# Low-rank products moved into the last pair of the first attention, latent norm applied as scales

## The reference

```python
u = rmsnorm(h, attn_norm_g)
proj = u @ w_in                       # 3*512 + 256 + 128 + 64 columns
q_sb, k_sb, v_sb, c_q, c_kv, k_rope = split(proj)
# 8 heads of 64: stick-breaking attention on q_sb, k_sb, v_sb
# latent attention, 4 heads: 128 plain and 64 rotated columns in q and k, 128 in v
q_m = rmsnorm(c_q, q_a_norm_g) @ w_q_b     # 256 -> 4 * (128 + 64)
kv  = rmsnorm(c_kv, kv_a_norm_g) @ w_kv_b  # 128 -> 4 * (128 + 128)
q_rope, k_rope = apply_rope(...)
s = (q_nope . k_nope + q_rope . k_rope) * MLA_SCALE, causal; p = softmax(s); o = p @ v
```

## Time and profile before

| | us |
|---|---|
| three runs | 3790.58, 3791.27, 3786.0 |
| median | 3790.58 |
| span of the profiled execution, first to last instruction | 3784.3 |
| own time of the profiled execution | not listed apart from the three runs |
| TensorE busy | 3616.2 (96% of the span) |
| VectorE, ScalarE, GpSimd busy | 1805.3, 1216.1, 1341.8 |
| mean granted TensorE clock | 0.980 of full speed |

### The profile page before, as it was taken

One profiled execution on the slowest core, in us unless ns is written; L12 is line 12 of the kernel. 1 busy time (PEld: TensorE's weight loads), 2 busy tenths in 40 slices (PEclk: granted clock), 3 DMA queues, 4 the chain that ended last, 5 costly groups with the idle time before them and its releaser, 6 DMA issues. The chain is left out here.

```text
span 3784.3 us, 48486 instructions
## 1 busy us (share of the span) xinstructions
PE 3616.2 (96%) x17484; PEld 2956.1 (78%) x17484; DVE 1805.3 (48%) x3405; ACT 1216.1 (32%) x2273; POOL 1341.8 (35%) x800
## 2 busy tenths in 40 slices
PE   7997898999999999999999999998999999999997
PEld 6776677888888888788888888886888686868686
DVE  4666544244444445566666666666303424242412
ACT  4777243200000003455545555556101202020200
POOL 3211201233333222565565566563333131313331
PEclk9997899999999999999999999998999999999998
DMA  3100101111111113432222422211413020202231
GB/s 95 29 12 6 42 31 73 56 62 46 49 50 50 46 34 79 56 52 51 53 51 48 37 40 36 37 37 56 150 51 100 28 73 23 78 23 73 95 133 67
DMA packets 201142, 208.81 MB, mean 55 GB/s; under 512 B 12479, under 2 KB 155886, under 8 KB 200958
## 3 DMA queue, kind: packets, MB, share of 16 engines
q1 hardware_dynamic: 181390, 155.23, 17.5%
q10 hardware_dynamic: 19568, 50.93, 3.7%
HBM read 174.61 MB, written 31.52 MB: 54 GB/s over the span
## 5 line engine op out<-in xcount | busy, mean ns | idle before, releaser
L877 PE MATMUL ps<-all_u_hi,kept_w_hi 128*128 128x512 f32 x1952 | 784.7, 402 | 1.8 <-PEq L486 1.8
L881 PE MATMUL ps<-all_u_hi,kept_w_lo 128*128 128x512 f32 x1952 | 763.1, 391 | 0.0
L880 PE MATMUL ps<-all_u_lo,kept_w_hi 128*128 128x512 f32 x1952 | 761.3, 390 | 0.0
L827 POOL CAST kept_w_hi<-kept_w_raw 128x1024 fp32r<-128x1024 f32 x116 | 127.2, 1096 | 1210.1 <-PE ps L877 710.5
L1554 POOL TENSOR_SCALAR even_probs<-even_probs,even_stat 128x640 f32<-128x640 f32 (+1 forms) x250 | 428.0, 1717 | 347.8 <-DVE even_stat L1995 347.8
L881 PEld LDWEIGHTS ps<-all_u_hi,kept_w_lo 128*128 128x128 f32 x1952 | 366.7, 188 | 79.2
L877 PEld LDWEIGHTS ps<-all_u_hi,kept_w_hi 128*128 128x128 f32 x1952 | 368.5, 189 | 67.9 <-POOL sb_w_lo L829 2.0
L880 PEld LDWEIGHTS ps<-all_u_lo,kept_w_hi 128*128 128x128 f32 x1952 | 368.1, 189 | 66.2
L1811 ACT ACTIVATE even_probs<-even_probs,even_stat 128x128 f32<-128x128 f32 (+7 forms) x256 | 199.1, 778 | 300.8 <-DVE even_stat L1989 300.8
L829 POOL TENSOR_TENSOR kept_w_lo<-kept_w_raw,kept_w_hi 128x1024 fp32r<-128x1024 f32 x116 | 285.3, 2459 | 9.3
L877 PE MATMUL ps<-kept_w_hi,all_u_hi 128*128 128x512 f32 x640 | 250.5, 391 | 7.6 <-DVEq L2874 7.2
(11 more groups left out here) (417 smaller groups left out, 7267.5 us busy)
## 6 DMA issues: line engine op xcount, KB each, us to landing
kept_w_raw<-in_even_w_in_dram SPq DMA_DIRECT2D x64, 512.0 KB, 7.4
kept_w_raw<-in_odd_w_in_dram SPq DMA_DIRECT2D x48, 512.0 KB, 3.8
kept_w_raw<-in_w_up_dram SPq DMA_DIRECT2D x16, 512.0 KB, 4.0
mlp_w_raw<-in_w_up_dram SPq DMA_DIRECT2D x16, 512.0 KB, 4.0
kept_w_raw<-in_w_down_dram SPq DMA_DIRECT2D x16, 512.0 KB, 3.5
mlp_w_raw<-in_w_down_dram SPq DMA_DIRECT2D x16, 512.0 KB, 3.5
scratch_h<-residual SPq DMA_DIRECT2D x8, 1024.0 KB, 4.6
residual<-scratch_negc ACTq DMA_DIRECT2D x16, 512.0 KB, 5.5
```

Source lines behind the costliest of these rows:

```text
L827: nc.gpsimd.tensor_copy(hi, raw).then_inc(w_hi.sem, 1)
L877: ins = nc.tensor.matmul(dst, lh, rh, start=first, stop=False)
L880: nc.tensor.matmul(dst, lh, rl, start=False, stop=False)
L881: return nc.tensor.matmul(dst, ll, rh, start=False, stop=last)
```

## The change

- `stick_stage` also runs the five low-rank units: `following(h)` no longer ends with the last pair, and `LAST_PIECES` gives pair 3 its 40 eighths, two in most steps. They use the same `DENSE` bank. Halves 0 to 5 (c_q, c_kv) are evicted by ScalarE into X[0..2]; halves 6 to 9 by VectorE (`rope_half`), which rotates the key at once.
- The angle chain and the two sines move to the opening of `stick_stage`; ScalarE loads the table for exp and ln behind its last eviction there.
- The latent weights are three more units in the raw slots of the attention's weights. Two are split into the slots of `w`, the third into tile 3 of `UH` and `UL` after the last dense product. Rotated columns are laid out by the loads (many DMAs of 32 or 64 columns) instead of GpSimd copies.
- The 12 identity transposes at the end of the stage, `low_stage` and `turn_norm_stage("nc")` are gone. Both latent gains join the first stage's gain loads (two more DMAs).
- `heads_stage` begins by splitting the unnormalised latents times gain (ScalarE `CH`, VectorE `CL`), squares them, sums the squares over partitions with 24 one-column matmuls between jobs 3 and 4, spreads the key root over partitions with 8 matmuls ahead of the key jobs, and has 5 banks for jobs in place of 8. Keys are evicted by VectorE with a multiplication by the spread root, values by ScalarE with a scale per position. The query root goes into the scale of the latent attention's exponential and its bound.

```diff
+        LAST_PIECES = [2] * STEPS
+        LAST_PIECES[3] = LAST_PIECES[9] = LAST_PIECES[15] = LAST_PIECES[21] = 1
+        LAST_PIECES[22] = LAST_PIECES[23] = 0
...
         def following(h):
-            p = h // STEPS + 1
-            return p if p < rounds else None
+            return h // STEPS + 1
...
+                sp.dma_start(pos, positions.rearrange("b s -> (b s)").partition_broadcast(P))\
+                    .then_inc(step_pos.sem, 16)
+                sp.dma_start(rf[:], tables["rope"]).then_inc(step_pos.sem, 16)
...
+                for v, unit in enumerate(low_units + latent_units):
+                    w_load(sp, w, rounds + v // per, per, v % per, unit)
...
+                first = per * (rounds + 1)
+                for n in (first, first + 1, first + 3, first + 4):
+                    split_unit(n)
+                split(first + 2, *latent_kv)
...
-                    for e in eighths_at(h) if nxt else ():
+                    for e in eighths_at(h):
                         if e % 4 == 0:
                             pe.wait_ge(dense_out.sem, dense_out.at(ND * nxt + e // 4))
...
                 weigh(3 * NCY - 1)
-                turn_ident(DENSE[:, 0:P], 12)
...
                     if n == 1:
                         split_of(0, 0, 0)
+                        act.wait_ge(step_dve.sem, step_dve.at(9))
+                        nc.scalar.activation(RS, A, ACT.Sin).then_inc(step_act.sem, 1)
                     elif n == 3:
                         split_of(0, 0, 1)
+                        act.wait_ge(step_dve.sem, step_dve.at(18))
+                        nc.scalar.activation(RC, B, ACT.Sin).then_inc(step_act.sem, 1)
+                load_exp_and_ln()
...
-                    if nxt and s:
-                        for e in eighths_at(h - 1):
-                            if e % 4 == 3:
-                                take_half(nxt, e // 4, DENSE)
+                    if s:
+                        for n in halves_ended(h - 1):
+                            if nxt < rounds or n not in ROPE_HALVES:
+                                take_half(nxt, n, DENSE)
...
+                def rope_half(n):
+                    i, half = divmod(n - 2 * per, 2)
+                    at = slice(half * HALF, (half + 1) * HALF)
+                    dve.wait_ge(dense_done.sem, dense_done.at(ND * rounds + n + 1))
+                    if i == 0:
+                        nc.vector.tensor_tensor(KR[:, at], DENSE, RC[:, at], ALU.mult).then_inc(dense_out.sem, 1)
+                        return
...
+                    nc.vector.tensor_tensor(TMP[:], DENSE, RS[:, at], ALU.mult).then_inc(dense_out.sem, 1)
...
+                    nc.vector.tensor_tensor(KR[:, at], KR[:, at], TMP[:], ALU.add).then_inc(rot_step.sem, 1)
```

In `heads_stage` (TensorE, then ScalarE, then VectorE):

```diff
+        PIECES = [(0, 0), (1, 0), (0, 1), (1, 1), (2, 0), (2, 1)]
...
-        BANKS = 8
+        BANKS = 5
+        SPREAD, SUMS = 5, 7
...
+                    pe.wait_ge(squares.sem, squares.at(LATENTS))
+                    for s, tiles in enumerate((range(QT), range(QT, LATENTS))):
+                        for t in range(TT):
+                            for k in tiles:
+                                last = nc.tensor.matmul(ps[:, SUMS, s * TT + t:s * TT + t + 1],
+                                                        SQ[:, k, t * P:t * P + P], ones[:, 0:1],
...
+                    if n == 4:
+                        sums_of_squares()
+                    if n == ON_DVE[0]:
+                        spread()
...
+                for k, half in PIECES:
+                    nc.scalar.activation(CH[:, k, at], C[:, k, at], ACT.Copy,
+                                         scale=gain_cols[:, 5 * KT + k:5 * KT + k + 1]).then_inc(hi_done.sem, 1)
+                for k in range(LATENTS):
+                    nc.scalar.activation(SQ[:, k, :], C[:, k, :], ACT.Square).then_inc(squares.sem, 1)
...
+                rope(0, 0)
+                rope(0, 1)
+                rope_lo(0)
+                dve.wait_ge(stats_done.sem, stats_done.at(1))
...
+                rstd_chain_dve(dve, v, r, q)
...
+                rope(1, 0)
+                rope(1, 1)
+                for t in range(TT):
+                    nc.vector.tensor_scalar(R[:, t * P:t * P + P], ident[:], KV_ROOT[:, t:t + 1], None, ALU.mult)\
+                        .then_inc(turn_scaled.sem, 1)
+                rope_lo(1)
+                nc.vector.tensor_tensor(KRL, KR[:], KRH.bitcast(F32), ALU.subtract).then_inc(split_lo.sem, 1)
+                for n in ON_DVE:
+                    dve.wait_ge(spread_out.sem, spread_out.at(half + 1))
+                    dve.wait_ge(dense_done.sem, dense_done.at(n + 1))
+                    nc.vector.tensor_tensor(KN[:, j, at], ps[:, n % BANKS, :], R[:, at], ALU.mult)\
+                        .then_inc(part_done.sem, 1)
```

In `latent_stage`:

```diff
-                    nc.scalar.activation(p, p, ACT.Exp, scale=MLA_SCALE, bias=nb[:, s], accum_out=tot[:, s])\
+                    nc.scalar.activation(p, p, ACT.Exp, scale=Q_SCALE[:, t:t + 1], bias=nb[:, s], accum_out=tot[:, s])\
...
-                    nc.vector.tensor_scalar(nb[:, s], top_[:, s], -MLA_SCALE, None, ALU.mult)\
+                    nc.vector.tensor_scalar(nb[:, s], top_[:, s], NEG_Q_SCALE[:, qt:qt + 1], None, ALU.mult)\
```

More of the change, by code:

```diff
@@ L462, in turn_norm_stage @@
         xt = resident if src is None else sb("x", [P, TT, W])
-        NG = NK + len(more) * KT
+        rows_of_more = [sum(n // P for n, _ in more[:i]) for i in range(len(more) + 1)]
+        NG = NK + rows_of_more[-1]
         gain_rows = sb("gain_rows", [NG, P])
@@ L952, in stick_stage @@
         ND = 2 * per
-        KN, QN, VN = (sb(name, [P, SEQ]) for name in ("k_next", "q_next", "v_next"))
+        KN, QN, VN, RC, RS = (X[:, i, :] for i in range(5))
         NEXT = (KN, QN, VN)
@@ L1354, in _ @@
                     s = h % STEPS
+                    if nxt == rounds and s:
+                        for n in halves_ended(h - 1):
+                            if n in ROPE_HALVES:
+                                rope_half(n)
                     if k == 0:
@@ new lines, in heads_stage, with rope_cols, q_cols @@
+    def heads_stage(stage, C, CH, CL, rope_w, nope_w, kv_w, KR, RC, RS, QR, TR, QN, KN, QRP, KRH, KRL, V):
+        ctx = ExitStack()
+        sb = allocator(ctx, stage)
+        SQ = sb("squares", [P, LATENTS, SEQ])
+        stat = sb("stat", [P, 3, 2 * TT])
+        v, ln, q = (stat[:, i, :] for i in range(3))
+        r = latent_roots
+        KV_ROOT = r[:, TT:2 * TT]
+        QT = Q_LORA // P
+        def rope_cols(i, it, k):
+            at = slice(((i * 2 + it) * 2 + k) * P, ((i * 2 + it) * 2 + k + 1) * P)
+            return tuple(W_[:, at] for W_ in rope_w)
+        def q_cols(k, h):
+            at = slice((k * MLA_HEADS + h) * NOPE, (k * MLA_HEADS + h + 1) * NOPE)
+            return tuple(W_[:, at] for W_ in nope_w)
@@ new lines, in _ @@
+                rope_hi(0)
+                act.wait_ge(mean_sq.sem, mean_sq.at(1))
+                nc.scalar.activation(ln, v, ACT.Ln).then_inc(ln_done.sem, 1)
+                act.wait_ge(ln_done.sem, ln_done.at(1))
+                nc.scalar.activation(r, ln, ACT.Exp, scale=-0.5).then_inc(root.sem, 1)
+                for i, n in enumerate(ON_ACT[:2 * MLA_HEADS]):
+                    take(n)
+                    if i == 2:
+                        rope_hi(1)
+                act.wait_ge(spread_done.sem, spread_done.at(1))
@@ L2400, in _ @@
+                for half in range(2):
+                    nc.scalar.activation(R[:, half * HALF:(half + 1) * HALF], ps[:, SPREAD + half, :], ACT.Copy)\
+                        .then_inc(spread_out.sem, 1)
+                act.wait_ge(newton.sem, newton.at(4))
+                for n in ON_ACT[2 * MLA_HEADS:]:
+                    take(n)
             @block.vector
             def _(dve):
-                dve.wait_ge(split_hi.sem, split_hi.at(1))
-                nc.vector.tensor_tensor(KRL, KR[:], KRH.bitcast(F32), ALU.subtract).then_inc(split_lo.sem, 1)
```

489 lines of the change are left out of this document (219 added, 270 removed).

## The result

The changed kernel takes **3743.9 us** (median of four runs, 3742.66 to 3745.87) where the kernel before took 3788.82 beside it (four runs, 3786.0 to 3791.27): a ratio of 0.9883, 95% interval 0.9871 to 0.9895. It is faster, by 44.9 us of the medians. The forecast was 3746.

A forecast was written before the change was run, and what follows sets the result against it. The prediction took TensorE, busy in 96% of the span, as the bound, with room in the last pair's waits for ScalarE. 46.1 us gained less 0.85 in the opening gave 3745.4, said as 3746; range 3735 to 3760.

The forecast's parts named there:

- Last pair, 101 us: Last attention pair with 40 eighths of low-rank products: 101 us, between 93 and 115, 30 more than before.
- The work term of 92.5: Last pair: TensorE's work alone, 38 us of attention and 54.5 of eighths, 92.5 us.
- The handovers, five to six at 8.8 us: Last pair: TensorE waits for evictions of the single DENSE bank where halves end mid-step, together 8.8 us.
- I cost it at nothing: Border before heads: GpSimd's last latent splits, 7 us, covered by 0 to 1 us; any barrier wait costed at nothing.
- Sums of squares ... I take 3.0: Heads: 24 one-column matmuls at 0.125 us each, 3.0 us, bounds nothing and 5.4.
- The clock at the start of heads, 2.3: Start of heads: first 12 matmuls at 1.2 GHz after TensorE idles some 6.5 us; 2.3 us charged.
- The opening, "Covered": Opening: angle chain from 38 to 64 hidden before softplus passes at 67.93; only loads and table show, 0.85 us.
- The lock of the two engines: Opening: VectorE's angle chain slowed beside GpSimd, ending 31 us late, 3777 us in all; chance 0.03.
- The eighths adding whole: Last pair: eighths lengthen a latency chain instead of filling waits, 134 us, 3779 in all; chance 0.1 beyond 113 us.
- Slower: Last pair: eighths add whole and all ten halves wait 4.1 us, 166.5 us, 3811 in all; chance 0.02.
- not reached: Removed stages behind the last pair: their work was hidden anyway, so no gain; chance below 0.01.
- Better than that: Last pair and heads: no late handover, no clock lost, 92.5 and 39 us, 3735 in all; chance 0.1.

The follow-up runs named there:

- aligned: Changed kernel with two eighths in each of steps 0 to 19 of the last pair and none in 20 to 23: 3740.51 us.
- sums_fr: Changed kernel with squares written as fp32r and summed in one block against two columns of fp32r ones: 3739.4 us.
- woven: Changed kernel with one sum-of-squares matmul behind each of 24 products of the second query rotations: 3742.83 us in float32, 3740.91 in fp32r.
- half_dense: Changed kernel with one of the two row blocks of each eighth in the last pair left out: one run of 3731.48 us.
- set one: Runs compared on one chip: changed kernel unedited (3746.53 us) and three edits of it, with the kernel before beside them.
- late_pool: Changed kernel with GpSimd's second key split and weight splits in the opening waiting for the end of VectorE's angle chain: 3744.51 us.
- three_parts: Changed kernel with aligned, sums_fr and VectorE's first query split moved ahead of the product with the sine table's sign: 3732.22 us.
- warm_three: three_parts with 30 and 10 identity transposes between last pair and heads, and 14 behind the latent attention's first scores: 3733.14 us.

## Why the forecast was right, and where it was not

**The direction and the mechanism held.** TensorE became the last pair's bound; the low-rank products took the place of waits and of half clock there. Working by the steps:

- *Last pair, 101 us:* 98.0. The work term of 92.5 stands (91.65 busy; 93.5 in all without late handovers). The handovers, five to six at 8.8 us, were 6.3 us in six. The place, the cause and the order's part in it are shown by aligned. The term was mis-sized by 2.5: the two that I put at 2.2 and 2.3 were 1.38 and 1.64, and the three at 1.1 were 0.69, 0.78 and 0.78.
- *"I cost it at nothing"* (GpSimd at the border): the cover of "0 to 1 us" was short by 1.3. Border 5.4, not 4.1; aligned brings back 4.1.
- *"Sums of squares ... I take 3.0":* 6.85, above the upper bound of 5.4. The failing step is reading the row "x8" of the earlier trace rows as eight matmuls. Each float32 matmul leaves two records; it was four, at 0.25 each. By 0.25 the term comes to 6.0. The spread has the same slip, 1.0 against 1.7. sums_fr shows that the price goes by the record. Sums, spread and clock (next point) together make up 6.0 of the 6.3 us by which heads took longer than forecast.
- *The clock at the start of heads, 2.3:* nine products, 9 x (0.45 - 0.227) = 2.0. What was missing is a second stretch at the lower clock, behind the one-column matmuls: 1.7 us; woven, it does not come. The Trainium skill, "TensorE: Matmul & The Clock Gate", section "What's actually happening", says that throttled is the default and activity releases it. I had applied this to the idle border alone; here the clock fell in and behind a block in which TensorE was busy in 6.85 of 6.85 us, which that sentence by itself does not foretell.
- *The opening, "Covered":* wrong. I had the chain "from 38 to 64" by a length of 25.9 us that has the product with the sign in it; it ran from 38.87 to 65.63, beside GpSimd, and with the sign to 67.52. But I checked it only against the softplus passes, and not what is queued behind it on VectorE: the split of the first queries, which the first scores await. The gain loads (0.67 at the last dense matmul) and the table (0.2) came out as put; the split added the rest, 2.06 in place of 0.85 by the last pair. The lock of the two engines, a rival at 31 us and a chance of 0.03, was this wait of 2 us in small.
- *The signs.* The forecast called itself wrong if the first softplus pass in the opening started more than 2 us later than before. It started 2.87 later: that sign came, and what it pointed at is the point above. "The sums of squares near 3 us" and "heads of 42 us" failed too, at 6.85 and 48.6. Those of the last pair held: TensorE busy in over 93% of the time at a clock of 0.98, no waits for ScalarE's rows, six handovers in 6.3 us.
- *Rivals.* The eighths adding whole is refuted by the pair itself and by half_dense. "Slower" and "not reached" fell with it. "Better than that" was not reached either; aligned shows its pair of 92.5, at 93.5.

**Two deviations nearly cancel.** The terms by themselves, as measured, give a stretch of 152.0 and an opening of 2.06: a gain of 39.5 us, not 45.2; the spans say 40.3, and behind the stretch the mask came 1.1 us sooner (3.6 us against 4.7). So the sum of terms was 5.7 us too hopeful. But medians fell by 44.9, and by 42.8 in set one. The two profiled executions are not typical ones: the kernel before was profiled in its fastest execution (3786.0, which is 2.8 under the median of its four) and the changed kernel in its slowest (3745.87, 2.0 over its median). These 4.8 us are the difference between 44.9 and the 40.1 by which the two executions differ. My step "and the median 6.3. What lies around the span doesn't change" took for one thing what was two: what lies around a span is 1.7 us before (3786.0 over 3784.3) and 1.9 after, and the other 4.6 are how far that execution lay under the median of the three. Which stage is slower in a usual execution of the kernel before is not shown, for it has no second profile. A gain of medians cannot be had from one execution to better than the spread of executions, 3782.66 to 3794.7 for the kernel before over all sets. So the mechanism held, and the number came close partly by luck.

## What to carry to other kernels

Before work is put beside a chain of waits, add up the bound engine's own work and charge each handover of a single buffer by the step in which it ends and the next begins; then lay the pieces so that no two meet, which here was worth 6 us for two lines. When an operation is "covered", ask who is queued behind it on its engine, and which other engine slows it. And count matmuls in the code, not records: here a float32 matmul left two and a float32 transpose one.

## What the runs showed of the hardware

- 24 float32 matmuls of one column, back to back, left 48 records and took 6.85 us at a mean granted clock of 0.76 and 5.27 us at 1.00: 0.29 and 0.22 us a matmul. 24 fp32r matmuls of two columns left 24 records and took 2.60 us, 0.108 each. Singly behind a product of 512 columns they cost 0.14 and 0.03, and the product 0.09 more. 18 float32 transposes left 18 records.
- Behind the block of float32 one-column matmuls, in which TensorE had no gap, the products started 0.43 apart (granted clock 0.50) as they do behind an idle border: 8 of them after 6.85 us and after 5.27, 13 in late_pool. Behind the fp32r block of 2.60 us it was 8 in sums_fr and three_parts, three products later in the one and at once in the other, and none in warm_three. With a product between each two there is none.
- VectorE's operations of 1024 columns took 0.69 us (one tensor in) and 1.23 (two) alone and up to 2.77 and 3.29 beside GpSimd's.
- A load of 512 KB, issued first at the start of a stage, was awaited for 3.3 to 5.2 us in executions of nearly the same code. Where TensorE then stood for 3.3 to 3.8 us, the four matmuls behind took 2.21 to 2.93 us; where it stood for 2.0 to 2.3, 1.56 to 2.39. It is one place where a microsecond or two gained ahead of it disappears.
